# Exchanging the low and high halves of a kernel's on-chip memory map

## What is computed

```python
for i in range(2):
    ul = modulate(rms_norm(hl, norm_mix_g[i]), sh1_l, sc1_l)      # latent, and the same for context
    oc, ol = even_mixer(uc, ul, ...) if i == 0 else odd_mixer(uc, ul, ...)
    hl = hl + g1_l * ol
    hl = hl + g2_l * sq_relu_mlp(modulate(rms_norm(hl, norm_ff_g[i]), sh2_l, sc2_l), w_ff1[i], w_ff2[i])
    # context tokens too, in layer 0 only
def sq_relu_mlp(x, w1, w2):
    return jnp.square(jax.nn.relu(x @ w1)) @ w2
```

## Time and profile before

| | us |
|---|---|
| median of 3 runs | 1292.99 (1292.24 to 1293.57) |
| the profiled execution, its own time | 1293.59 |
| its span in the trace | 1291.8 |
| TensorE matmul busy | 1206.2 (93%) |
| VectorE busy | 818.1 (63%) |
| ScalarE busy | 598.4 (46%) |
| GpSimd busy | 86.5 (7%) |
| mean granted clock of TensorE | 0.976 |

### The profile page before, as it was taken

One profiled execution on the slowest core, in us unless ns is written; L12 is line 12 of the kernel. 1 busy time (PEld: TensorE's weight loads), 2 busy tenths in 40 slices (PEclk: granted clock), 3 DMA queues, 4 the chain that ended last, 5 costly groups with the idle time before them and its releaser, 6 DMA issues.

```text
span 1291.8 us, 18257 instructions
## 1 busy us (share of the span) xinstructions
PE 1206.2 (93%) x6894; PEld 979.4 (76%) x6894; DVE 818.1 (63%) x1179; ACT 598.4 (46%) x1005; POOL 86.5 (7%) x73
## 2 busy tenths in 40 slices
PE   5799899999998999899999999997989897999998
PEld 3466578787876787687887887885777567999997
DVE  3653479696977564677585675795442785756664
ACT  4421154655647331741331321424969774644552
POOL 0000100101010005000000000053000003000000
PEclk9799999999999999899999999998989999999999
DMA  9555212111211124353454443531233003455553
GB/s 358 205 230 210 95 50 66 60 55 50 66 66 34 65 94 158 112 195 113 165 195 136 167 167 130 206 137 63 98 115 119 28 2 131 161 182 179 179 180 128
DMA packets 41529, 166.27 MB, mean 129 GB/s; under 512 B 4480, under 2 KB 6656, under 8 KB 38400
## 3 DMA queue, kind: packets, MB, share of 16 engines
q1 hardware_dynamic: 41184, 164.97, 36.3%
q10 hardware_dynamic: 288, 0.54, 0.1%
HBM read 164.45 MB, written 1.05 MB: 128 GB/s over the span
## 4 chain that ended last, share of the span: by engine, by line
PE 71%; DVE 13%; ACT 7%; issue 4%; DMA 3%; DVEq 0%; SPq 0%; ACTq 0%
PE ps L1564 54%; PE ps L1571 8%; DMA mring<-in_w_mod 2%; DVE cacc L1297 2%; PE ps L1587 1%; DVE sm L1516 1%; ACT ey L1037 1%; ACT u L933 1%; DVE ey L1371 1%; ACT w_hi L883 1%; DVE macc L1440 1%; DVE prob L1541 1%; DVE mixF L1397 1%; PE ps L1724 1%; DMA xload<-in_ctx 1%
## 5 line engine op out<-in xcount | busy, mean ns | idle before, releaser
L883 ACT ACTIVATE w_hi<-raw 128x1024 fp32r<-128x1024 f32 x206 | 216.7, 1053 | 244.4 <-DMA raw<-in_w_ff 186.6
L1148 DVE TENSOR_TENSOR w_lo<-raw,w_hi 128x1024 fp32r<-128x1024 f32 x206 | 257.2, 1248 | 113.5 <-ACT w_hi L883 113.2
L1564 PE MATMUL ps<-a_hi,w_hi 128*128 128x512 f32 (+1 forms) x868 | 321.1, 370 | 0.5 <-DVE w_lo L1148 0.5
L1564 PE MATMUL ps<-a_hi,w_lo 128*128 128x512 f32 (+1 forms) x868 | 309.4, 356 | 0.0
L1564 PE MATMUL ps<-a_lo,w_hi 128*128 128x512 f32 (+1 forms) x868 | 309.3, 356 | 0.0
L1564 PE MATMUL ps<-b_hi,w_hi 128*128 128x512 f32 (+1 forms) x560 | 192.9, 344 | 0.0
L1564 PE MATMUL ps<-b_hi,w_lo 128*128 128x512 f32 (+1 forms) x560 | 192.7, 344 | 0.0
L1564 PE MATMUL ps<-b_lo,w_hi 128*128 128x512 f32 (+1 forms) x560 | 192.5, 344 | 0.0
L1564 PEld LDWEIGHTS ps<-a_hi,w_hi 128*128 128x128 f32 x868 | 165.4, 191 | 29.2 <-issue 3.9
L1564 PEld LDWEIGHTS ps<-a_lo,w_hi 128*128 128x128 f32 x868 | 165.5, 191 | 25.4 <-issue 1.2
L1564 PEld LDWEIGHTS ps<-a_hi,w_lo 128*128 128x128 f32 x868 | 165.1, 190 | 23.5
(11 more groups left out here) (237 smaller groups left out, 1487.6 us busy)
## 6 DMA issues: line engine op xcount, KB each, us to landing
raw<-in_w_ff SPq DMA_DIRECT2D x128, 512.0 KB, 3.3
mring<-in_w_mod SPq DMA_DIRECT2D x24, 1024.0 KB, 7.7
mring<-in_w_mod SPq DMA_DIRECT2D x32, 768.0 KB, 4.9
raw<-in_w_in_even SPq DMA_DIRECT2D x36, 512.0 KB, 3.3
raw<-in_w_in_odd SPq DMA_DIRECT2D x18, 512.0 KB, 3.3
raw<-in_w_out_even SPq DMA_DIRECT2D x16, 512.0 KB, 3.3
raw<-in_w_out_odd SPq DMA_DIRECT2D x8, 512.0 KB, 3.3
bias<-in_rpb_na SPq DMA_DIRECT2D x8, 256.0 KB, 3.7
```

What stands on the lines that cost most here:

```text
L883: nc.scalar.activation(w_hi[:, u % RING, :, :], raw[:, u % RING, :, :], ACT.Copy).then_inc(hi_done, 1)
L1148: v.tensor_tensor(w_lo[:, u % RING, :, :], raw[:, u % RING, :, :], w_hi[:, u % RING, :, :].bitcast(F32), ALU.subtract).then_inc(lo_done, 1)
L1564: ins = mm(out_ap, w_[:, n % RING, k, :], (x_[k][:, 0:ntok] if type(x_) is list else x_[:, k, 0:ntok]), start=(k == 0 and j == 0), stop=(k ...
```

## The change

The stage region gets a fixed size, 114304 bytes, and its place right behind `a_lo`. The weight ring, the constants and the small tiles are placed after it. After them, `at[0] = out_at` goes back, and the stage region's tiles are placed as before, relative to the new `out_at`; an assertion says that they end before the ring.

```diff
+STAGE_BYTES = 114304
...
         a_lo = place("a_lo", [P, KT, T], F32R)
+        out_at = at[0]
+        at[0] = out_at + STAGE_BYTES
         raw_at = at[0]
         raw = place("raw", [P, RING, KT, P])
         w_hi = place("w_hi", [P, RING, KT, P], F32R)
...
         xstat = place("xstat", [P, 2, NCH])
-        out_at = at[0]
+        at[0] = out_at
 
         mixF = place("mixF", [P, 2 * KT, T])
         region = at[0]
...
         dts = {n: place("dt_" + n, [P, NCH, 2 * NH]) for n in ("dt", "dta", "ea", "dte", "tot")}
+        assert at[0] <= raw_at
```

## The result

The changed kernel takes 1297.2 us (median of 11 executions, 1296.1 to 1298.5); the kernel before, run beside it, 1292.2 (11 executions, 1287.1 to 1293.6). The ratio is 1.0045, with a 95% interval of 1.0035 to 1.0055: slower by 4.5 to 7.1 us. The forecast was 1301, slower, with a range of 1285.5 to 1303.5.

What follows compares the result with a forecast made beforehand. TensorE's matmul pitch was taken as the bound. At 512 columns on `a`, ff1's +4.1 us and the other products' +3.7 us gave +7.8 on 1293.0, all else zero: 1301 us, range 1285.5 to 1303.5.

Steps and rivals of the forecast that it cites:

- The direction and the mechanism: Ring's 512-column matmuls: pitch depends on moving and stationary tile together, so `a` loses its settled 227 ns; slower, chance 0.52.
- both rivals: Moving tile alone decides: 1286, chance 0.30. Gap not of place, or gains offset losses: 1293 give or take 2, chance 0.18.
- The term for `a`: Settled 512-column matmuls on `a`, about 1570, each go from 226.7 to 232 ns, 5.3 ns more: +7.8 us.
- Ahead of the MLP: Products before layer 0's MLP: 540 settled matmuls, plus about 110 in outA, lose 5.3 ns each; about a fifth before outA hidden.
- the upper end of the sum: Same matmuls on `a`, if their pitch goes to 233 ns instead of 232: +9.9 us.
- `b`: 960 matmuls on `b` at 512 columns stay at 232 to 233 ns: between -1 and 0 us, taken as 0.
- The 256-column matmuls: 1536 matmuls in layer 1's MLP: taken as zero, bound 1% of one pass, 0.4 us either way.
- the likeliest case's own range: Whole kernel, if the slower forecast of 1301 holds: 1299 to 1303.5 us.
- The base: Whole kernel before the change: median of the runs, 1293.0 us, from which the forecast counts.
- ScalarE, VectorE and transfers at zero: Other engines and DMA: no effect of place; bounds under 1 us for the engines, 0.5 us for transfers.
- L1659: Product streaming `a` past high 48-column weights: 231 ns, never settling, taken as evidence against the moving tile alone deciding.
- rival 1: Moving tile alone decides: 960 matmuls on `b` speed up from 233.3 to 226.7 ns, total 1286 us, chance 0.30.

Runs made afterwards that it cites:

- run 1: Changed kernel with the weight ring and all above it 384 bytes higher, so weights and activations rest equally: 1288.9 us, 0.9981 of the kernel before.
- run 4: Kernel before with the ring 128 bytes higher and the stage region 512 in all, so `b` matches the weights and `a` does not: 1293.8 us, 1.0025.
- run 5: Kernel before with everything 128 bytes higher, the stage region 128 more, and the weights of L1659 padded from 48 to 64 columns: 1288.0 us, 0.9985.
- run 3: Kernel before with the stage region 128 bytes higher, so `b` rests at 384 by 512, equal to the ring only by 256: 1288.4 us, 0.9985.
- run 2: Kernel before with the stage region 384 bytes higher, so `b` rests at 128 by 512 like the ring: 1289.15 us, 0.9982.
- run 12: Kernel before with the ring 64 bytes higher and the stage region 128 in all, moving tiles 64 bytes behind the weights by 256: 1296.7 us, 1.0054.
- run 8: Kernel before with `w_hi` alone 128 bytes higher and `b` kept at rest 0 by 256: 1297.0 us, 1.0047.

## Why the prediction was right, and where its sizes were off

*The direction and the mechanism* were right: the pitch depends on moving and stationary tile together. Runs 1, 4 and 5 show it against both rivals, and run 3 settles what the forecast left open: by 256, not by 512. Why a distance should cost anything, no run shows.

*The term for `a`* was 1570 x 5.3 = 8.3 us, 7.8 on the path. The pitch went from 227.5 to 232.5 (232 was taken) on 1880 matmuls, 9.3 us gross. Per pass of layer 0 the chain gives 0.9 us with `b`'s gain in it; the forecast had 4.1 / 4 = 1.0. That part was right. Ahead of the MLP the forecast had 540 + 110 matmuls x 5.3 ns less a fifth, 2.8 us. The pair of traces is 2.2 us apart there, which looks close but is luck: the 1.2 us that it was ahead by chance and the 1.6 us of the clock's fall nearly cancel in it. From 160 us to the first MLP the matmuls' pitches add up to 3.7 us more, and the chain is longer by 1.7: more matmuls were settled than forecast, and half of what they lost, not a fifth, fell into waits. These two sizes were off in opposite directions. And the upper end of the sum is wrong as it stands: 233 instead of 232 gives +9.9 only if nothing falls into waits; with the fifth taken off, as for the other two, it is +9.3.

*`b`* was "between -1 and 0, I take 0": -0.6 ns x 939 = -0.6 us.

*The 256-column matmuls* are the step that failed: "I take zero", because "matched `a` and unmatched `b` differ by 1 to 2% there in either direction between windows". They do not differ in either direction: the earlier trace rows had 127 for the matched tile and 129 for the unmatched. Read straight, the first is the slower one, and unmatching `a` should gain 1% of its 256-column time. It did, 119.8 to 118.7 on 1065 matmuls, 1.2 us; `b`'s 0 to 0.5 us on top is not the change's for sure, since the second trace of the kernel before has it too. The bound of 0.4 us per pass, 1.6 in all, did hold this, but was not carried into the likeliest case's own range, 1299 to 1303.5, which misses 1297.2.

*The base.* 1293.0 was the median of three executions. The kernel before came out at 1292.2 beside the changed one, and at 1289.7 to 1290.8 beside the experiments. Counted as a difference, the forecast was +8 and the result +5.0 in medians, +5.8 by the ratio. With the 256-column and `b` terms, +7.8 - 1.2 - 0.6 = +6.0. That this meets +5.8 so well is in part luck, with the term ahead of the MLP too large by 1 us. The clock may have made up for it: the changed kernel's executions had 0.976 in the mean, those of the kernel before, beside the experiments, 0.977 to 0.978, and by run 2 (5.1 us for 0.006) that is about 1 us, an estimate. The runs don't separate the two.

*ScalarE, VectorE and transfers at zero*: 1052 for 1053 ns, 692 for 692, `mring` 7.6 us for 7.7 and `raw` 3.3 for 3.3 to landing. The Trainium skill says that the first transaction of a descriptor which begins off a multiple of 256 bytes starts at the 256-byte boundary below it (DMA: Bandwidth & Descriptors, how a descriptor splits into AXI transactions). By that `mring` and `raw` each cost one transaction more in one of the two kernels. That moved nothing here, and `raw` at rest 192 in run 12 takes 3.3 us too.

*The evidence.* L1659 tipped the choice between my forecast and rival 1, and run 5 shows that it had another cause: at equal rests it takes 233 ns, with 48 columns of weights, where "fewer weights should cost less". What does hold it there was not tested. The other reason, that `a` and the ring shared a rest and `b` and `mixE` didn't, was the sound one. 0.52 was a fair chance for it; with L1659 struck out it should have been nearer to even with 0.30.

*The rule against it* was that TensorE's two read ports are independent and it never waits (the Trainium skill, SBUF — State Buffer, who interferes with whom). What the prediction drew from it, one pitch for every tile, is contradicted: same instructions, same order, same data, and a pitch between 227.0 and 233.3 ns at 512 columns, 113.3 and 120 at 256, by offsets alone. That the two reads meet is a likely reading; run 8 didn't pin it down.

## What to carry to other kernels

In a kernel whose chain is an unbroken run of matmuls, compare the pitch of every moving tile with that of the others at the same width, and look up the rests of tile and weights by 256: a difference of 2% is then a matter of placing, not of instructions. There is no one good distance, since 512 and 256 columns want different ones, so try the four distances for each width, and where one tile serves both widths, shift its columns for one of them. And when two tiles of the trace differ in two windows, believe the sign even where the size is small.

## What the runs showed of the hardware that I had not expected

- At 256 columns equal rests are the slowest choice of the four (120.0 ns), and weights that begin 64 bytes further on give 113.3, 5.6% less. The sign of the distance counts: 64 the other way gives 117.8.
- The same distance of 192 is the slowest at 512 columns, if by little (233.3 ns, 232.5 to 233.2 at 128).
- The pitch of a tile that doesn't match can differ from one execution to the next (`b` at 256 columns, 119.3 and 118.7), while `a`, matched, repeats (227.4 to 227.5 and 119.8).
- A faster stretch can lengthen the next wait, and a fall of the granted clock can come behind it: 6.35 us of lead became 4.12 within 28 matmuls in run 2. The wait grew to 2.1 us in all eight traces with the faster `b`, and the fall followed in five.
